# Attention half of a two-layer decoder step: blocks by one store and four loads, weights ahead of value pages, normalisations around row 7's maxima

## What is computed

```python
s = jnp.einsum('bqhd,bkhd->bhqk', qi, k_all).astype(jnp.float32) * scale
logits = jnp.where(mask, s + (c_q[..., :, None] - c_t[..., None, :]), -jnp.inf)
p = jax.nn.softmax(logits, axis=-1)
return jnp.einsum('bhqk,bkhd->bqhd', p.astype(v_all.dtype), v_all)
...
q, gate = jnp.split(rms_norm(x, norm_g) @ w_in, 2, axis=-1)
q = rms_norm(q.reshape(bsz, t, B_HEADS, B_DH), q_norm)
o = forgetting_attention(q, k_all, v_all, c_all)
o = o.reshape(bsz, t, B_WIDTH).astype(x.dtype) * jax.nn.silu(gate)
return x + o @ w_o
```

## Time and profile before

| what | before |
|---|---|
| median of 3 runs | 1576.83 us (1570.41 to 1579.2) |
| the profiled execution | 1576.44 us |
| its span, first to last instruction | 1574.7 us |
| TensorE busy, granted clock | 1498.9 us (95%), 0.991 |
| VectorE, ScalarE, GpSimd busy | 1008.6, 684.7, 421.4 us |
| chain that ended last | PE 74%, DMA 8%, DVE 6%, issue 4%, ACT 4%, POOL 3% |
| SP queue | 258.75 MB, 53.0% of 16 DMA engines' span |

### The profile page before, as it was taken

One profiled execution on the slowest core, in us unless ns is written; L12 is line 12 of the kernel. 1 busy time (PEld: TensorE's weight loads), 2 busy tenths in 40 slices (PEclk: granted clock), 3 DMA queues, 4 the chain that ended last, 5 costly groups with the idle time before them and its releaser, 6 DMA issues.

```text
span 1574.7 us, 23177 instructions
## 1 busy us (share of the span) xinstructions
PE 1498.9 (95%) x8353; PEld 1101.0 (70%) x8353; DVE 1008.6 (64%) x1987; ACT 684.7 (43%) x1380; POOL 421.4 (27%) x335
## 2 busy tenths in 40 slices
PE   6999999999999999999999898989999898988998
PEld 6888888888888864447776666767666676754443
DVE  5869687786968672235575766757677576756421
ACT  4445554444555442122464454535445453635100
POOL 5022212122221000021333435143342524323200
PEclk9999999999999999999999999999999999999999
DMA  9582936648293733323356575776757578588641
GB/s 275 168 252 80 273 114 196 200 124 254 78 274 133 228 123 99 90 87 109 96 178 218 170 247 192 242 254 195 257 168 237 201 232 277 184 300 323 209 147 55
DMA packets 289411, 296.81 MB, mean 188 GB/s; under 512 B 25722, under 2 KB 247098, under 8 KB 289298
## 3 DMA queue, kind: packets, MB, share of 16 engines
q1 hardware_dynamic: 278162, 258.75, 53.0%
q0 software_dynamic: 11136, 36.59, 6.9%
HBM read 239.90 MB, written 122.50 MB: 230 GB/s over the span
## 4 chain that ended last, share of the span: by engine, by line
PE 74%; DMA 8%; DVE 6%; issue 4%; ACT 4%; POOL 3%; SPq 1%; DVEq 0%; POOLq 0%
PE psum L2106 36%; PE psum L2130 7%; PE psum L2613 7%; DMA arena<-in_w_kv 4%; PE psum L2183 3%; PE psum L2413 3%; DMA block_rows<-arena 2%; PE psum L2439 2%; PE psum L2069 2%; PE psum L2373 1%; DVE arena L474 1%; PE psum L2471 1%; DMA arena<-block_rows 1%; DVE arena L1790 1%; PE psum L2420 1%
## 5 line engine op out<-in xcount | busy, mean ns | idle before, releaser
L2106 PE MATMUL psum<-arena 128*128 128x252 f32 (+1 forms) x3472 | 816.2, 386 | 0.9 <-DVE arena L1426 0.9
L2106 PEld LDWEIGHTS psum<-arena 128*128 128x128 f32 x3472 | 645.0, 191 | 121.5 <-issue 26.0
L934 POOL TENSOR_TENSOR arena<-arena 128x1024 f32<-128x1024 f32 x64 | 152.9, 2390 | 369.0 <-DMA arena<-k_pages 364.4
L1426 DVE TENSOR_TENSOR arena<-arena,psum 128x252 f32<-128x252 f32 (+1 forms) x310 | 129.1, 417 | 173.0 <-PE psum L2106 155.8
L2613 PE MATMUL psum<-arena 128*128 128x512 f32 x256 | 115.7, 604 | 6.0 <-DVE arena L1836 3.7
L1009 ACT COPY arena<-psum 128x252 f32<-128x252 f32 (+1 forms) x124 | 46.2, 373 | 158.5 <-PE psum L2106 158.4
L2130 PE MATMUL psum<-arena 128*128 128x512 f32 x256 | 113.0, 594 | 0.1
L2613 PEld LDWEIGHTS psum<-arena 128*128 128x128 f32 x256 | 47.7, 192 | 64.1 <-issue 57.0
L1251 ACT ACTIVATE arena<-psum,arena 128x128 f32<-128x128 f32 (+3 forms) x64 | 33.2, 523 | 134.7 <-DVE arena L1773 134.7
L2413 PE MATMUL psum<-arena 64*128 64x512 f32 (+3 forms) x384 | 79.6, 518 | 9.2 <-DVE arena L1790 9.0
L2130 PEld LDWEIGHTS psum<-arena 128*128 128x128 f32 x256 | 47.5, 190 | 57.4 <-issue 56.5
(11 more groups left out here) (267 smaller groups left out, 2172.3 us busy)
## 6 DMA issues: line engine op xcount, KB each, us to landing
k_pages<-in_cache_k SPq DMA_DIRECT2D x64, 512.0 KB, 6.6
v_pages<-in_cache_v SPq DMA_DIRECT2D x64, 512.0 KB, 7.3
arena<-k_pages SPq DMA_DIRECT2D x64, 512.0 KB, 8.3
arena<-v_pages SPq DMA_DIRECT2D x64, 512.0 KB, 6.0
arena<-in_w_in_a SPq DMA_DIRECT2D x32, 512.0 KB, 6.8
arena<-in_x_prompt SPq DMA_DIRECT2D x16, 512.0 KB, 8.1
arena<-in_w_kv SPq DMA_DIRECT2D x16, 512.0 KB, 8.6
arena<-in_w_in_b SPq DMA_DIRECT2D x16, 512.0 KB, 9.5
```

The costliest lines, as they stand in the source:

```text
L934: pool.tensor_tensor(k_ring[:, m % 2], k_ring[:, m % 2], q_all[:, m % S:m % S + 1, :].broadcast_to([P, PAGES, P]), ALU.mult).then_inc(kq_m ...
L1426: dve.tensor_tensor(out, more, bank[n % 2][:, 0:size(u)], ALU.add).then_inc(of.by_dve, 1)
L2106: ins = pe.matmul(bank[n % 2][:, 0:size(u)], w[:, k, :], x[:, k, :], start=(k == 0 and r in (0, 1, 3, 4)), stop=(k == HK - 1), skip_group_ ...
```

## The change

- `store_row` writes all 128 partitions with one transfer (a row of 4n floats each) instead of four transfers of 32 partitions that also regroup; `load_row` regroups instead, with four transfers into 32 partitions each. `MOVES` and the waits on `rows_stored` follow.
- SP's `pair`: key page m - 2 moves into the pair before, ahead of `load_row(p, 7)` (as `k_in(m + 6)`); value and gate weights are issued ahead of key page m and the value pages; the high forget sums of pair p follow the value pages; the low sums of the next pair move from the pair's start to behind `v_in(p, 0)`, in front of row 5's store. `last` follows, and the residual rows move ahead of row 4's store.
- VectorE: `gate_in` ahead of `fin(p, 1)`; `turn_blocks(p, 4)` ahead of `score(m + 1)`; `norm(p + 1, 0)` ahead of row 7's maxima and `norm(p + 1, 1)` behind them; the two block turns of row 7 stand together.

```diff
-MOVES = 16
-STORES = 4 * 16
+MOVES = 4 * 16
...
             def hi_in(p):
+                if p:
+                    sp.wait_ge(max_done, 2 * TT * p)
                 sp.dma_start(c_hi, c_dram[1, 2 * p:2 * p + 2].rearrange("x n -> (x n)").partition_broadcast(P)).then_inc(hi_loaded, 16)
...
-                n = block_len(i)
-                dst = block_rows[i - LOW_ROWS, :, 0:4 * n].rearrange("(r l) (g n) -> g l r n", r=4, g=4)
-                for g in range(4):
-                    src = weights[32 * g:32 * g + 32, 0:4 * n].rearrange("p (r n) -> p r n", r=4)
-                    sp.dma_start(dst[g], src).then_inc(rows_stored, 16)
+                n = 4 * block_len(i)
+                sp.dma_start(block_rows[i - LOW_ROWS, :, 0:n], weights[:, 0:n]).then_inc(rows_stored, 16)
...
-                sp.wait_ge(rows_stored, STORES * high_row(p, i))
+                sp.wait_ge(rows_stored, 16 * high_row(p, i))
...
-                src = block_rows[i - LOW_ROWS, :, 0:4 * n].rearrange("p (g n) -> p g n", g=4)
-                sp.dma_start(dst, src).then_inc(pt_moved, 16)
+                src = block_rows[i - LOW_ROWS, :, 0:4 * n].rearrange("(g l) (r n) -> r l g n", g=4, r=4)
+                for r in range(4):
+                    sp.dma_start(dst[32 * r:32 * r + 32], src[r]).then_inc(pt_moved, 16)
 
             def pair(p):
                 m = S * p
                 if p:
-                    sp.wait_ge(max_done, 2 * TT * p)
-                lo_in(p + 1)
-                if p:
-                    k_in(m - 2, m - 1)
-                    v_in(p - 1, 1)
-                    k_in(m)
+                    k_in(m - 1)
                 sp.wait_ge(b_units.done, vg_b(p, 14))
                 load_wb(sp, w_v, w_kv_d, p + 1, 1, w_v_loaded)
                 load_wb(sp, w_g, w_qg_d, p + 1, 1, w_g_loaded)
                 if p:
+                    k_in(m)
+                    v_in(p - 1, 1)
+                    hi_in(p)
                     k_in(m + 1)
                 k_in(m + 2, m + 3)
                 store_row(p, 4)
                 load_row(p, 4)
                 if p:
                     v_in(p, 0)
+                    sp.wait_ge(max_done, 2 * TT * p)
+                lo_in(p + 1)
...
                 store_row(p, 7)
+                k_in(m + 6)
                 load_row(p, 7)
-                sp.wait_ge(max_done, 2 * TT * (p + 1))
-                hi_in(p + 1)
 
             def last():
 
                 p, m = PAIRS - 1, S * (PAIRS - 1)
+                k_in(m - 1)
+                sp.wait_ge(max_done, 2 * TT * p)
                 w_ob_in(early_b, 2)
...
-                k_in(m - 2, m - 1)
+                k_in(m)
                 v_in(p - 1, 1)
-                k_in(m)
+                hi_in(p)
...
+                resb_in(0)
+                resb_in(1)
                 store_row(p, 4)
                 load_row(p, 4)
                 v_in(p, 0)
                 k_in(m + 4)
-                resb_in(0)
-                resb_in(1)
...
                 row_max(p, 4)
+                gate_in(p)
                 fin(p, 1)
                 kq(6)
                 if p:
                     shift(p - 1, 1)
-                gate_in(p)
+                turn_blocks(p, 4, 0, 1)
                 score(m + 1)
-                turn_blocks(p, 4, 0, 1)
...
+                if nxt:
+                    norm(p + 1, 0)
                 row_max(p, 7)
+                if nxt:
+                    norm(p + 1, 1)
                 vg(5)
                 fin(p, 2)
                 if nxt:
                     top_of(p, 0)
-                    norm(p + 1, 0)
                 vg(6)
                 last(3)
                 if nxt:
                     shift(p, 0)
-                turn_blocks(p, 7, 0)
-                if nxt:
-                    norm(p + 1, 1)
-                turn_blocks(p, 7, 1)
+                turn_blocks(p, 7, 0, 1)
```

More of the change, by code:

```diff
@@ L1784, in turn_blocks @@
                 if high_row(p, i) > 1:
-                    dve.wait_ge(rows_stored, STORES * (high_row(p, i) - 1))
+                    dve.wait_ge(rows_stored, 16 * (high_row(p, i) - 1))
                 n = block_len(i)
```

## The result

| what | before | after |
|---|---|---|
| median, side by side (20 runs each) | 1575.42 us (1568.46 to 1584.89) | 1585.08 us (1573.12 to 1591.15) |
| ratio to before, 95% interval | 1 | 1.0057 (1.0038 to 1.0076) |
| the profiled execution, its span | 1576.44, 1574.7 us | 1584.62, 1582.9 us |
| TensorE busy, granted clock | 1498.9 us, 0.991 | 1501.5 us, 0.984 |
| chain that ended last | PE 74%, DMA 8% | PE 69%, DMA 16% |

The account below looks back on a forecast made before the run. TensorE's waits were taken to bound the kernel: row turns 23.7 us, value product 13.0, scores 9.0. Gains 17.5 + 8.0 + 1.5 + 2.3 + 3.5 = 32.8 us off 1576.4 gave 1543.6, median 1544; range 1524 to 1566.

Parts of the forecast that it names:

- Weights ahead of value pages: Row 3's turns: 17.5 us of waits and 8.0 us of clock gained in pairs 1 to 5, 1.5 us in pair 6.
- Rival D: Row 3: the weights' own time is the wait; 0.9 to 1.6 us left per pair, 1546 to 1549, inside main case's 0.66.
- What moves behind the weights, and the gate and row 4's turns: Value pages, high sums, key page delayed on SP; VectorE reordered: cost 0, or 0.4 us a pair if the gate is slow.
- Key page in pair 7: Page issued earlier for GpSimd; TensorE's 2.28 us wait behind VectorE in pair 7 goes: gain 2.3 us.
- Normalisations: VectorE, around row 7's maxima: row 7's two block turns stand together and end 1.55 us earlier.
- the terms of travel in row 7's chain: Store and load terms within a chain netted to about -0.5 us per boundary, 3.5 us gained; bounds -3 and +1.8.
- one store instead of four: Row 7's store, from first issue to landing: 6.3 us becomes 4.3 us.
- row 6's four loads in front of it: Row 6's load takes 2 us longer, still queued when row 7's store is issued: counted +0.3 us.
- row 7's load, undivided: Key page's 0.5 MB ahead of row 7's blocks: +0.8 us of its 1.3 us, the rest in store-to-load latency.
- row 7's load in four: Row 7's load in four transfers of 32 partitions: 5.7 us becomes 7.3 us.
- Rival A: Row 7's chain 1.8 us longer, loads meeting store and key page: 1560, or 1571 with 1.6 us clock per wait; chance 0.16.
- C: One store no faster, loads slower: up to 5.7 us later per boundary plus 1.7 us of clock, 1598; chance 0.06.

Follow-up runs that it names:

- kernel 9: Before, with one edit: value and gate weights issued ahead of key page m and the value pages. 0.982, 1549.07 us.
- kernel 12: After, with four stores and one load again, key page behind row 7's load, low forget sums at the pair's start. 0.9723, 1533.69 us.
- kernel 10: Before, with VectorE's edits alone: gate, row 4's turns, the two normalisations, row 7's turns together. 0.989, 1562.03 us.
- kernel 5: After, with each row's blocks loaded by one transfer to all 128 partitions, regrouping left out. 0.9765, 1541.63 us.
- kernel 8: After, with row 7's load in four pieces, rows 4 to 6 each loaded by one transfer without regrouping. 0.9916, 1565.72 us.
- kernel 2: Before, with only the block travel changed: one store, four loads. 1.0093, 1593.17 us.
- kernel 1: After, with the old travel: four regrouping stores and one load, all else as changed. 0.9862, 1555.91 us.
- kernel 11: After, with four stores and one load and the key page behind row 7's load; low sums as changed. 0.9782, 1542.33 us.
- kernel 3: After, with key page m + 6 issued behind row 7's four loads instead of ahead. 1.0033, 1582.31 us.
- kernel 7: After, with the four loads in the order of partitions 0, 64, 32, 96. 1.0018, 1579.35 us.
- kernel 6: After, with four loads over all 128 partitions, a quarter of the columns each, regrouping left out. 0.9893, 1560.28 us.

## Why the prediction was wrong, step by step

*Weights ahead of value pages: right.* 17.5 us of waits, 8.0 us of clock and 1.5 us in pair 6 make 27 us; done alone it brought 28 us (kernel 9). In after, row 3's turns and the next unit take 1.04 and 1.87 us where the earlier trace rows had 1.97 and 2.50: 1.56 us, for the 1.6 taken. The landing of the weights fell from a median of 9.0 us to

```profile
DMA to landing us min/median/max: 4.0/6.9/9.3
```

and VectorE waits for them nowhere. Rival D is thus out.

*What moves behind the weights, and the gate and row 4's turns: cost nothing*, as far as kernel 12 (0.969 to 0.975) against kernels 9 and 10 together (0.971) can tell.

*Key page in pair 7: right.* TensorE's 2.28 us there are gone from its list of waits; 2.0 us for the output weights have come up in other places.

*Normalisations: right in kind, low in size.* The turn's 1.55 us in seven pairs would be 10.9 us; done alone, VectorE's edits brought 14 to 17 us (kernel 10). By the prediction most of this gain was to be eaten by other terms of the same chain.

*The failed step: the terms of travel in row 7's chain, above all row 6's loads ahead of row 7's store.* The prediction netted the whole chain to 0.5 us shorter at each boundary, with a bound of +1.8; its terms from the store's issue to the product come to +0.7. Measured are +3.6 us in pair 3 and +4.0 us in the mean of pairs 1 to 6. From before and kernels 5 and 8 the terms are:

| term | foreseen | pair 3 | mean of pairs 1 to 6 |
|---|---|---|---|
| one store instead of four (before, kernel 5) | -2.0 | 6.28 to 4.63: -1.65 | 6.1 to 5.1: -1.0 |
| row 6's four loads in front of it (kernel 8, after) | +0.3 | 4.64 to 6.68: +2.04 | 5.4 to 6.9: +1.6 |
| row 7's load, undivided (before, kernel 5) | +0.8, for the key page | 5.73 to 7.42: +1.69 | 5.7 to 7.0: +1.3 |
| row 7's load in four (kernel 5, after) | +1.6 | 7.42 to 8.93: +1.51 | 7.0 to 8.9: +2.0 |
| sum from store to product | +0.7 | +3.59 | +4.0 |

The means don't add up to the tenth, as the second row is taken from kernel 8 and the others from kernel 5.

The largest miss is row 6's loads, given 0.3 us where they cost 1.6 to 2.0. The prediction had seen them "still in the queue when row 7's store is issued" and yet counted almost nothing. The store's gain was rightly sized for a queue that is free: in pair 0 of kernel 2 it lands after 3.9 us, where the four pieces before took 6.1 us, and 4.3 was foreseen. But in the changed order VectorE turns row 7 as soon as row 6 is stored, so the store follows the issue of row 6's load by 2.4 us and meets its data even when that is undivided. The load in pieces was nearly right. For the key page alone kernels 1 and 11 are the cleaner pair, as they differ in nothing else: 0.8 us in pair 3 and 1.1 us in the mean. So its term was about right beside an undivided load, and beside four loads the page cost nothing (kernel 3); the rest of the third row is not shown to be the page's. The mistake in method was to discount what stood ahead because part of it would lie beside something else, without a row that showed this. SyncE's queue is one line, and at this place it is nearly full: in after, the DMA share from 1116 to 1126 has a mean of 0.94.

The sum's bounds don't follow from its terms either. With the +2.5 us that the prediction itself gives for store and load if only the load changes, they add up to +2.45 and not +1.8; with its -2.0 they add up to -2.05 and not -3. And 1 MB (1.05 million bytes) at 203 GB/s takes 5.2 us, not 4.7.

A second term was missing from the main case: that a longer wait at row 7 would lose the clock that row 3 got back. Rival A priced it, at 1.6 us each. In after six of row 7's products are slow, by 1.4 to 2.8 us each, and so is that of rows 4 and 5 in pair 7 (2.3 us); before has one slow product (1.65 us, in pair 0). That makes the 12.4 us. Of the 39.8 us that the product lost, 12.4 us are clock.

*Which rival it was.* By mechanism, A: the loads in pieces meet row 7's store and the key page. By size, C: that said "slower" would begin at about 3 us more in the chain plus the clock, and at 4.0 us more from store to product it did. C's own reason, an undivided store that is no faster, was wrong. With its bound too narrow, A left the slower side too little chance.

*What the prediction said would show it wrong* did: the blocks' wait passed 30 us, and VectorE waits at the block turns for the store (23.9 us).

By the Trainium skill (SBUF — State Buffer, section "Door 1: The DMA port swizzle (why `[64,N]` ≈ `[32,N]`)") a transfer that touches 32 partitions reaches half of the ports, and partitions 0 to 63 share one half and 64 to 127 the other. The trace agrees in direction, as kernels 5 and 8 show: 221 to 254, and 321 in the last window, against 349 to 385 GB/s, with other transfers in both. In the crossed order of kernel 7 neighbours in the queue lie in different halves by that mapping; it brought 0.4%, within the intervals, so putting them there doesn't recover the loss.

*What stays open.* Why four loads over all partitions (kernel 6) cost 1.3% over one was not found out; the packets are the same. In every kernel that was run, pieces of 32 partitions also regroup and all others don't, so the two were never taken apart: one load that regroups in itself wasn't tried, nor four loads of 32 partitions without regrouping, nor two loads instead of four. And why the key page's place does nothing beside four loads, and costs 1.1 us beside one, is not shown.

## What to carry to other kernels

Where two engines meet once in each turn of a loop, write the loop's time as the sum of a chain from one meeting to the next, and add up what an edit puts into that chain. A wait removed elsewhere is a gain only as far as this chain doesn't grow: with the old travel row 3's 28 us arrived in full (kernel 9), with the new one they were eaten, and the clock was lost at the new place. For every transfer ahead of the awaited one, work out when it lands: what is still in the queue at the issue of the awaited one is paid for, as row 6's pieces were (1.6 to 2.0 us), unless a row shows that it isn't, as for the key page beside four loads. And test each half of a bundle alone: here 2.8% of gain was hidden by one edit of the data's path and two of the order.

## What the runs showed of the hardware that was not expected

**Pieces fill the DMA engines with less.** A DMA share of 1.0 to 1.1 went with 221 to 254 GB/s in three windows of kernel 8 (loads of 32 partitions), and one of 0.94 to 1.12 with 349 to 385 GB/s in kernel 5 (the undivided load), with packets of the same sizes. The share tells that the engines are taken, not that they move much.

**The clock after a wait of 2 to 3 us goes either way.** These are products of kernels 11 and 5, with the wait in brackets:

```profile
1019.93 5.18 PE L2442 MATMUL psum<-arena 128*64 128x256 f32 x32 [2.01 <-DMA arena<-block_rows]
```

```profile
1367.71 3.53 PE L2438 MATMUL psum<-arena 128*64 128x256 f32 x32 [2.78 <-DMA arena<-block_rows]
```

The shorter wait cost 1.65 us of clock and the longer one nothing. Of the waits over 3 us of kernels 1, 2 and after, all were followed by a slow product (4.9 to 6.4 us). Waits of 1.9 us and less in front of row 7's product were followed by a fast one (3.53 us) in all kernels.
